# Final RMS norm of a hybrid block: where the gains are kept, in which order the last products run, and which engine scales

## The reference, cut to what matters

```python
def rms_norm(x, g):
    y = x * lax.rsqrt(jnp.mean(x * x, axis=-1, keepdims=True) + EPS)
    return y * g

x = x + mixed @ w_out          # (512, 2048) + (512, 2048) @ (2048, 2048)
return rms_norm(x, g_final)    # g_final: 2048 gains, one for each column
```

## Time and profile before

| what | us |
| --- | --- |
| median of 3 runs | 1173.29 |
| lowest, highest | 1172.86, 1174.75 |
| the profiled execution's own time | 1172.99 |
| its span, first to last instruction | 1171.1 |
| PE busy | 1129.4 |
| DVE busy | 731.7 |
| ACT busy | 432.8 |
| POOL busy | 38.6 |
| last matmul ends, from the span's start | 1150.25 |

### The profile page before, as it was taken

The page is one execution under the profiler, slowest core; times in us unless marked ns, Lnnn a source line. Parts: engine busy times, 40 slices in busy tenths (PEclk is TensorE's granted clock), DMA queues, the critical chain, the costliest instruction groups (busy, mean ns, idle before and its releaser), DMA issues.

```text
span 1171.1 us, 13456 instructions
## 1 busy us (share of the span) xinstructions
PE 1129.4 (96%) x5381; PEld 933.9 (80%) x5381; DVE 731.7 (62%) x1231; ACT 432.8 (37%) x572; POOL 38.6 (3%) x44
## 2 busy tenths in 40 slices
PE   5999999999999999999999999999999999999992
PEld 4999888888787788888777777888888887887882
DVE  5886568999655546428688886343243543957556
ACT  7423333332265443232222323333322322734454
POOL 4000000000000000000000000000000000000000
PEclk9999999999999999999999999999999999999996
DMA  7344543556533136755455564543775431677563
GB/s 251 105 111 108 150 138 111 141 108 151 137 112 104 37 108 139 162 125 153 117 165 139 128 154 113 164 144 129 160 154 118 108 106 58 221 257 257 185 210 144
DMA packets 188631, 166.35 MB, mean 142 GB/s; under 512 B 12868, under 2 KB 162712, under 8 KB 187928
## 3 DMA queue, kind: packets, MB, share of 16 engines
q1 hardware_dynamic: 167584, 129.97, 38.1%
q0 software_dynamic: 12800, 33.56, 12.6%
q10 hardware_dynamic: 8184, 1.95, 0.8%
HBM read 159.17 MB, written 37.75 MB: 168 GB/s over the span
## 4 chain that ended last, share of the span: by engine, by line
PE 82%; DVE 13%; ACT 3%; DMA 1%; issue 1%; ACTq 0%; SPq 0%; DVEq 0%
PE banks L502 21%; PE banks L503 21%; PE banks L504 21%; PE banks L747 4%; PE banks L749 4%; PE banks L748 4%; DVE w_lo L1135 2%; DVE score L1241 2%; DVE small L1240 2%; PE banks L654 2%; PE banks L635 1%; DVE score L1229 1%; DVE res L1576 1%; PE banks L704 1%; PE banks L644 1%
## 5 line engine op out<-in xcount | busy, mean ns | idle before, releaser
L502 PE MATMUL banks<-act_hi,w_hi 128*128 128x512 f32 (+1 forms) x1088 | 421.7, 388 | 2.7 <-DVE w_lo L1135 2.7
L504 PE MATMUL banks<-act_hi,w_lo 128*128 128x512 f32 (+1 forms) x1088 | 416.8, 383 | 0.0
L503 PE MATMUL banks<-act_lo,w_hi 128*128 128x512 f32 (+1 forms) x1088 | 416.7, 383 | 0.0
L1135 DVE TENSOR_TENSOR w_lo<-w_raw,w_hi 128x2048 fp32r<-128x2048 f32 x80 | 183.2, 2290 | 96.3 <-ACT w_hi L812 95.4
L502 PEld LDWEIGHTS banks<-act_hi,w_hi 128*128 128x128 f32 x1088 | 204.3, 188 | 43.0 <-DVE w_lo L1135 4.3
L504 PEld LDWEIGHTS banks<-act_hi,w_lo 128*128 128x128 f32 x1088 | 204.2, 188 | 38.0
L503 PEld LDWEIGHTS banks<-act_lo,w_hi 128*128 128x128 f32 x1088 | 204.5, 188 | 34.9
L812 ACT ACTIVATE w_hi<-w_raw 128x2048 fp32r<-128x2048 f32 (+1 forms) x81 | 154.2, 1904 | 99.7 <-DMA w_raw<-in_w_in 99.5
L1551 DVE TENSOR_TENSOR w_lo<-w_raw,w_hi 128x512 fp32r<-128x512 f32 (+1 forms) x64 | 68.3, 1090 | 48.2 <-ACT w_hi L1052 48.0
L1052 ACT ACTIVATE w_hi<-w_raw 128x512 fp32r<-128x512 f32 (+1 forms) x64 | 59.9, 950 | 73.0 <-DMA w_raw<-w_sums 46.4
L1563 DVE TENSOR_TENSOR gate<-gate,yb 128x512 f32<-128x512 f32 x16 | 11.1, 692 | 83.4 <-ACT gate L818 83.4
(11 more groups left out here) (287 smaller groups left out, 1437.6 us busy)
## 6 DMA issues: line engine op xcount, KB each, us to landing
w_raw<-in_w_in SPq DMA_DIRECT2D x68, 1024.0 KB, 5.8
w_sums<-in_w_out POOLq DMA_DIRECT2D x24, 1024.0 KB, 8.3
w_raw<-w_sums SPq DMA_DIRECT2D x32, 512.0 KB, 4.1
w_sums<-w_sums POOLq DMA_DIRECT2D x8, 1024.0 KB, 11.4
w_raw<-in_w_att_out SPq DMA_DIRECT2D x8, 1024.0 KB, 5.4
w_raw<-in_w_out SPq DMA_DIRECT2D x16, 512.0 KB, 4.5
xt<-in_x SPq DMA_DIRECT2D x4, 1024.0 KB, 8.0
w_raw<-in_w_ssm_out SPq DMA_DIRECT2D x4, 1024.0 KB, 5.2
```

The costliest lines, as they stand in the source:

```text
L502: nc.tensor.matmul(out_ap, wh, x_hi[k], start=(j == 0), stop=False)
L503: nc.tensor.matmul(out_ap, wh, x_lo[k], start=False, stop=False)
L504: last = nc.tensor.matmul(out_ap, wl, x_hi[k], start=False, stop=(j == n - 1))
L1135: v.tensor_tensor(w_lo[:, u % SLOTS, :], w_raw[:, u % SLOTS, :], w_hi[:, u % SLOTS, :].bitcast(F32), ALU.subtract).then_inc(split_done, 1)
```

## The change

- `g_last` moves from `uT` to region r3, over the parts `s_hi` of the first pass. SP loads it behind the two loads of block 24, with a wait until block 19 has used `s_hi`.
- DVE multiplies the left halves by the gains in blocks 29 (tokens 0 and 1) and 30 (tokens 2 and 3), behind the low parts of that block.
- The products of blocks 30 and 31 run by pairs of indices: first (2, 0) of both blocks for both tb, then (1, 3) of both blocks. Tokens 2 and 3 are thus complete first, and the token order is 2, 3, 0, 1.
- DVE adds for tokens 2 and 3, finishes token 2, adds for tokens 0 and 1, and finishes 3, 0 and 1.
- ACT squares a right half in one operation of 1024 (the last token in two of 512), takes the means of tokens 2, 3 and 0 and one root before the first part is ready. Columns 162 + 4t are set to zero at first, since a mean may be taken without a square there.
- The right half is finished by one DVE operation, (res x scale) x gains, in place. `fin` and ACT's scaling go.
- POOL scales the left half, in place, when the scale is ready. `square_out` moves to the place of `fin`.

```diff
@@ @@ SP
-            sp.wait_ge(shared_added, 16)
-            sp.dma_start(g_last[:, :], g_final.rearrange("(a d) -> a d", a=1).to_broadcast([P, D])).then_inc(gf_loaded, 16)
+                if n == 3 * HALF_K:
+                    sp.wait_ge(q_done, done_at(2 * HALF_K + QUADS - 1, 2, 1))
+                    sp.dma_start(g_last[:, :], g_final.rearrange("(a d) -> a d", a=1).to_broadcast([P, D])).then_inc(gf_loaded, 16)
@@ @@ POOL
+            pool.wait_ge(first_scaled, 2 * TOK)
+            for i, t in enumerate(LAST_TOKENS):
+                pool.wait_ge(scale_ready, i + 1)
+                pool.tensor_scalar(res[:, t, 0:HALF], res[:, t, 0:HALF], small[:, 188 + t:189 + t], 1.0, ALU.mult, ALU.mult).then_inc(final_done, 1)
@@ @@ PE
-            for tb in range(2):
+            for which, pair in enumerate(LAST_PAIRS):
                 for n in (BLOCKS - 2, BLOCKS - 1):
-                    pe.wait_ge(q_split, 2 * n + 2)
-                    for i in LAST_ORDER:
-                        second_pass(n, i, tb).then_inc(q_done, 1)
+                    pe.wait_ge(q_split, 2 * n + which + 1)
+                    for i in pair:
+                        for tb in range(2):
+                            second_pass(n, i, tb).then_inc(q_done, 1)
@@ @@ ACT
+            def root_of_last(i):
+                t = LAST_TOKENS[i]
+                link(nc.scalar.activation(square_out[:, 0:2, :].rearrange("p a n -> p (a n)"), res[:, t, HALF:D], ACT.Square,
+                                          accum_out=small[:, 176 + t:177 + t]))
+                root_of(t).then_inc(squares_done, 1)
+
+            act.wait_ge(first_scaled, 2 * TOK)
+            for t in LAST_TOKENS[:-1]:
+                link(mean_of(t))
+            t_last = LAST_TOKENS[-1]
+            link(nc.scalar.activation(small[:, 176 + t_last:177 + t_last], small[:, 163 + 4 * t_last:164 + 4 * t_last], ACT.Sqrt))
+            act.wait_ge(part_ready, 3)
+            root_of_last(0)
+            act.wait_ge(part_ready, 4)
+            root_of_last(1)
+            act.wait_ge(part_ready, 6)
+            link(square_of(t_last, 2, 162 + 4 * t_last))
+            link(mean_of(t_last))
+            act.wait_ge(part_ready, 7)
+            root_of_last(2)
+            act.wait_ge(part_ready, 8)
+            link(square_of(t_last, 3, 176 + t_last))
+            root_of(t_last).then_inc(squares_done, 1)
@@ @@ DVE
-            dve.wait_ge(gf_loaded, 16)
-            dve.wait_ge(first_squared, 2 * TOK)
-            for t in range(TOK):
-                v.tensor_tensor(res[:, t, 0:HALF], res[:, t, 0:HALF], g_last[:, 0:HALF], ALU.mult).then_inc(first_scaled, 1)
+                if n >= BLOCKS - 3 and n < BLOCKS - 1:
+                    dve.wait_ge(gf_loaded, 16)
+                    for t in (2 * (n - BLOCKS + 3), 2 * (n - BLOCKS + 3) + 1):
+                        dve.wait_ge(first_squared, 2 * t + 2)
+                        v.tensor_tensor(res[:, t, 0:HALF], res[:, t, 0:HALF], g_last[:, 0:HALF], ALU.mult).then_inc(first_scaled, 1)
@@ @@ DVE, finish(i)
                 v.reciprocal(small[:, 188 + t:189 + t], small[:, 184 + t:185 + t]).then_inc(scale_ready, 1)
                 dve.wait_ge(scale_ready, i + 1)
-                v.tensor_scalar(res[:, t, 0:HALF], res[:, t, 0:HALF], small[:, 188 + t:189 + t], None, ALU.mult).then_inc(final_done, 1)
+                v.scalar_tensor_tensor(res[:, t, HALF:D], res[:, t, HALF:D], small[:, 188 + t:189 + t], g_last[:, HALF:D], ALU.mult, ALU.mult
+                                       ).then_inc(final_rest_done, 1)
+
+            for tb in range(2):
+                bank = last_bank(tb, 2)
+                add_part(2 + tb, HALF + 512, bank).then_inc(part_ready, 1)
+                mark = add_part(2 + tb, HALF, bank, ALU.subtract)
+            link(mark)
+            for tb in range(2):
+                add_part(2 + tb, HALF, last_bank(tb, 0)).then_inc(part_ready, 1)
             finish(0)
+            for tb in range(2):
+                add_part(tb, HALF, last_bank(tb, 1)).then_inc(part_ready, 1)
+            for tb in range(2):
+                add_part(tb, HALF + 512, last_bank(tb, 3)).then_inc(part_ready, 1)
+            for i in range(1, TOK):
+                finish(i)
```

More of the change, by code:

```diff
@@ L157, in hybrid_kernel @@
         uT = at("uT", uT_at, [QUADS, SEQ])
-        g_last = at("g_last", uT_at, [D])
         ident = at("ident", region(KB // 2), [P])
@@ L227, in hybrid_kernel @@
         res = at("res", r2, [TOK, D])
-        fin = at("fin", r1, [2, HALF])
-        square_out = at("square_out", r1 + 8 * KB, [2, SEQ])
+        square_out = at("square_out", r1, [3, SEQ])
         ya_r = at("ya_r", r1, [KD, SEQ], F32R)
@@ L244, in hybrid_kernel @@
         s_lo = at("s_lo", r3 + 8 * KB, [QUADS, SEQ], F32R)
+        g_last = at("g_last", r3, [D])
         o[0] = r3
@@ L329, in hybrid_kernel @@
         PE_ORDER = ((0, 1, 2), (0, 2, 1, 3))
-        LAST_ORDER = (2, 0, 1, 3)
+        LAST_PAIRS = ((2, 0), (1, 3))
         SPLIT_AT = {2: [(0, 5), (0, 6)], 3: [(0, 7)], 4: [(1, 0), (1, 1)], 5: [(1, 2), (1, 3)], 6: [(1, 4), (1, 5)], 7: [(1, 6), (1, 7)]}
         SPLIT_ORDER = [(0, k) for k in range(5)] + [which for n in sorted(SPLIT_AT) for which in SPLIT_AT[n]]
-        LAST_TOKENS = (2, 0, 3, 1)
+        LAST_TOKENS = (2, 3, 0, 1)
         a_banks, b_banks, c_banks, d_banks = banks[0:2], banks[2:4], banks[4:6], banks[6:8]
@@ L1071, in _ @@
             high_of_first(4)
[L1073 to L1077, removed]
             def square_of(t, n, col):
@@ L1102, in _ @@
             act.wait_ge(first_squared, 2 * TOK)
[L1103 to L1114, removed]
@@ L1115, in _, with mean_of, root_of @@
-            scale_half(TOK - 1)
+            def mean_of(t):
+                return nc.scalar.activation(square_out[:, 2, 0:4], small[:, 160 + 4 * t:164 + 4 * t], ACT.Copy, scale=1.0 / D,
+                                            accum_out=small[:, 180 + t:181 + t])
+            def root_of(t):
+                return nc.scalar.activation(small[:, 184 + t:185 + t], small[:, 176 + t:177 + t], ACT.Sqrt, bias=small[:, 180 + t:181 + t],
+                                            scale=1.0 / D)
@@ L1553, in _ @@
             for t in range(TOK):
+                v.memset(small[:, 162 + 4 * t:163 + 4 * t], 0.0)
                 v.memset(small[:, 163 + 4 * t:164 + 4 * t], EPS * D).then_inc(first_scaled, 1)
@@ L1629, in _ @@
                     take_first_half()
-            dve.wait_ge(gf_loaded, 16)
-            dve.wait_ge(first_squared, 2 * TOK)
-            for t in range(TOK):
-                v.tensor_tensor(res[:, t, 0:HALF], res[:, t, 0:HALF], g_last[:, 0:HALF], ALU.mult).then_inc(first_scaled, 1)
+                if n >= BLOCKS - 3 and n < BLOCKS - 1:
[3 more added lines that the diff above has]
+                        v.tensor_tensor(res[:, t, 0:HALF], res[:, t, 0:HALF], g_last[:, 0:HALF], ALU.mult).then_inc(first_scaled, 1)
             def last_bank(tb, i):
-                dve.wait_ge(q_done, 2 * quarter_at(BLOCKS - 2) + 8 * tb + 4 + LAST_ORDER.index(i) + 1)
+                which = i not in LAST_PAIRS[0]
+                dve.wait_ge(q_done, 2 * quarter_at(BLOCKS - 2) + 8 * which + 4 + 2 * LAST_PAIRS[which].index(i) + tb + 1)
                 return (d_banks, a_banks, b_banks, c_banks)[i][tb]
[L1640 to L1667, removed]
             def finish(i):
@@ L1674, in finish @@
                 dve.wait_ge(scale_ready, i + 1)
-                dve.wait_ge(first_scaled, 2 * TOK)
-                v.tensor_scalar(res[:, t, 0:HALF], res[:, t, 0:HALF], small[:, 188 + t:189 + t], None, ALU.mult).then_inc(final_done, 1)
-            dve.wait_ge(shared_added, 16)
-            late_tokens(0)
-            early_tokens(0)
-            finish(0)
[L1682 to L1686, removed]
+                v.scalar_tensor_tensor(res[:, t, HALF:D], res[:, t, HALF:D], small[:, 188 + t:189 + t], g_last[:, HALF:D], ALU.mult, ALU.mult
[7 more added lines that the diff above has]
+                add_part(2 + tb, HALF, last_bank(tb, 0)).then_inc(part_ready, 1)
+            finish(0)
+            for tb in range(2):
[4 more added lines that the diff above has]
+                finish(i)
 _INS = ["x", "positions", "g_norm", "w_in", "b_merge", "a_re", "a_im", "log_dt", "ssm_b_re", "ssm_b_im", "ssm_c_re",
```

## The result

The changed kernel took 1166.09 us (median of 4 runs, 1165.59 to 1166.56); the kernel before 1173.07 (4 runs, 1172.86 to 1174.75). The ratio is 0.9937, 95% interval 0.9921 to 0.9953: 7 us faster, where 1166.3 was forecast. The profiled execution took 1165.59 with a span of 1163.7, so 1.89 lies outside it, as before; it is the shortest of the four.

What follows compares the result with a forecast made beforehand. PE bounds the kernel until 1150, then a 21 us tail of DVE, ACT and stores, held by g_last's late load and multiplications. Span 1171.1 - 6.9 = 1164.2, plus 2.19 gives 1166.3 us; range 1164.0 to 1168.8.

Steps and rivals of the forecast that it cites:

- Part 1: g_last's load at block 24: block 25's second load 0.3 late of 1.35 slack; load and four multiplications cost nothing.
- Rival (b): Block 24: g_last's load delays block 25 as res loads did, PE stalls 1.4; time 1167.7; chance 0.12.
- Part 2: PE's last 16 products reordered: same count, same 0.68 us each, every split needed no earlier than before.
- Part 3: Additions in the tail: eight multiplications (5.5 us of DVE) and ACT's four scalings go; DVE starts at 1142.8.
- Part 4: The finish: per token one DVE scalar_tensor_tensor, 1.22, and POOL's scaling of the first half, 1.04, taken as excluding each other.
- dear end: In the finish, POOL and DVE wait for each other each time: 1.22 + 1.04 + some 0.05.
- Rival (a): In the finish, POOL and DVE overlap freely; span 1162.9, time 1165.1; chance 0.20.
- (c): In the finish, a POOL operation has a large fixed part, 1.89 for 1024 as for 2048; time 1168.2; chance 0.12.
- (d): Slower than before: POOL, its scalar read for each partition, becomes the bound; 1176.3 at 4.61 an operation; chance 0.03.
- Part 5: Last six stores leave from 1154.05, take 1.9 + 3.15 / 0.40 = 9.8, plus 0.4 to the end: 1164.2.
- Sum: Whole kernel: span 1171.1 - 6.9 = 1164.2, plus 2.19 gives 1166.3, 0.6% faster than 1173.3.
- Rival (e): Tail: the early root does not keep ACT's table, 1.28 loads stay before each token's root; 1168.9; chance 0.06.

Runs made afterwards that it cites:

- part 1 alone: The kernel before with only the early load of g_last and the early multiplications by it: 1169.17 us, ratio to before 0.9962.
- two copies: The changed kernel with a second, unused copy of the gains loaded directly behind the first at block 24: 1168.02 us, one run.
- old order: The changed kernel with PE's last 16 products as before and tokens in the order 2, 0, 3, 1: 1166.45 us, ratio to before 0.9936.
- two kernels: The changed kernel with POOL only filling zeros, 1166.39 us, and with DVE's scalar_tensor_tensor left out, 1164.13 us; one run each.
- late last token: The changed kernel with three additions on spare data in front of the last token's reciprocal: 1167.24 us, one run.

## Why the prediction was right, point by point

- **What bounds it.** DVE's late start behind the gains was a link of the chain: part 1 alone, without the rest of the change, takes 3.7 off the tail, as it was worth by the rows (1146.5 to 1142.8).
- **Part 1, the load.** Forecast: block 25's second load 0.3 late, slack 1.35, no stall. Measured: issue to landing 4.2 instead of 3.7. In the changed kernel ACT saves the a banks at 1106.19; shifted by PE's 0.28 that is 0.5 later than in the earlier trace rows. Right, with the term a little small; so was that of block 25's first load, 1.4 late in the forecast and 1.9 measured (5.5 against 3.6). Rival (b) is what two copies do, at about its size: 3.0 us late (6.7 against 3.7) and a stall of 1.6, where the forecast took 2.7 and 1.4 from the res loads. Neither load nor multiplications cost PE anything: 51.26 from block 25's first load to the last matmul in both kernels.
- **Part 2.** The order cost nothing and, as the old order shows, brings nothing.
- **Part 3.** First addition to token 3's scale: 1142.53 to 1151.3, 8.8; forecast 1142.8 to 1151.7, 8.9.
- **Part 4.** The open price, POOL beside DVE, was taken at its dear end, and two kernels show that this is its mechanism: 1.82 and 1.95 against 1.28, 2.13 against 1.12. The sizes were each a little small (1.22 was 1.28, 1.04 was 1.12; with the fixed part of 0.15 that the forecast names it would even be 1.02) and the step from token to token was a little large: 2.25 and 2.35 in the forecast, 2.06 measured, as the two records need less than their sum. The total doesn't feel this, since the stream begins with the first of the three tokens: 2.35 from token 3's scale to its store in the forecast, 1151.31 to 1153.61 = 2.30 measured. Rival (a) would have given the same overlap for the fill and for the scaling; it falls. So do (c) and (d), by 1.12 alone.
- **Part 5.** Stores set the end: forecast 10.2 from the first of the last six to the end, measured 10.1, and unchanged when the last token came 1.5 later. The forecast gave them 1.3 in hand (ready at 1158.7, taken at 1160); the pause with the late last token says about 1.1. The stream has no gap and begins at 1153.61, as the forecast wanted.
- **Sum.** Span 1164.2, measured 1163.7: 0.3 of the difference is PE's end, of which the forecast knew nothing, 0.1 the stretch from the first addition to token 3's scale, and 0.1 token 3's left half and the stores. The median then lies 0.5 above the profiled execution where 0.3 was added, so 1166.09 is a little nearer to 1166.3 than the span is to its forecast. That is luck, and so is an agreement within a few tenths of a microsecond, since PE's end alone differs by up to 2.2 between executions. Rival (e) is out: the table load stands once, at 1139.75, ahead of the additions.

```profile
1139.75 1.28 ACT L1122 ACT_TABLE_LOAD   x1
1141.04 0.20 ACT L1122 ACTIVATE small<-small 128x1 f32<-128x1 f32 x1
```

Why PE's end differs by 2 us between executions of kernels that are the same up to block 24 stays open. The waits at blocks 16 and 17 (1.1 to 2.5 us) don't account for it: they are 1.5 in the changed kernel's first profile and 1.1 in its second, which ends 0.6 later. All of it, but for the stall with two loads, arises before block 25's loads, and up to 1.7 of it in the first 65 us.

## What to carry to other kernels

When a tail ends in stores, ask when the stream of stores begins and whether it pauses, not when the last engine is done: the end follows from its start plus bytes over rate. Before giving an idle engine a share of the work, ask what runs beside it; POOL reading SBUF beside a DVE operation with two tensors there took turns with it. To tell a part of the change from a shift that was there before it, measure from an event just ahead of the change and not from the start of the span. A load moved out of the tail has a price where it goes, and that price is found by looking at the nearest wait that its neighbours feed, here a copy behind them in ACT's queue and not the weights themselves.

## What the runs showed of the hardware that was not expected

- POOL filling 128x1024 (0.95) and DVE's scalar_tensor_tensor (1.28) overlap fully; POOL scaling the same tile, 1.12 alone and 1.13 beside additions with one tensor in PSUM, stretches to 2.08 to 2.21 and DVE's scalar_tensor_tensor to 1.82 to 1.95. In turn they need 2.06 for a token, less than the 2.40 of their sum.
- A scalar_tensor_tensor of 128x1024 takes 1.28, a multiplication of two tensors of that size 1.22, four of them 4.63.
- One megabyte of gains in the queue makes a load issued 2.3 us behind it land 1.9 us later and one issued 5.1 behind it 0.5; two megabytes make it 4.5 and 3.0.
- Three megabytes of stores, six in a stream, took 10.0 to 10.1 us from the first one's issue to the end of the span in nine profiles.
